# The second block's up stage with stationary weights, and matmuls of one size in a row

## The reference, cut to what matters

```python
# first block
h = rms_norm(x, ffn_norm_g)
a, g = jnp.split(h @ w_up, 2, axis=-1)           # 2048 x 11264
a = causal_dwconv(a, conv_w, conv_b)             # three taps along the rows
x = x + (gelu(a) * g) @ w_down
...
# second block
gu = rms_norm_2(x, norm_ffn) @ w_gate_up         # 2048 x 11264
gate, up = gu[..., :5632], gu[..., 5632:]
x = x + (silu(gate) * up) @ w_down_2
```

## Time and profile before

| | |
|---|---|
| median of 3 runs | 2599.71 us (2599.69 to 2600.31) |
| profiled execution | 2599.74 us, of it the span of the trace 2598.1 us |
| TensorE busy | 2586.1 us, 100% of the span |
| VectorE, ScalarE busy | 1474.3 us (57%), 1221.4 us (47%) |
| granted TensorE clock, mean | 0.999 |

### The profile page before, as it was taken

The page is one execution under the profiler, slowest core; times in us unless marked ns, Lnnn a source line. Parts: engine busy times, 40 slices in busy tenths (PEclk is TensorE's granted clock), DMA queues, the critical chain, the costliest instruction groups (busy, mean ns, idle before and its releaser), DMA issues.

```text
span 2598.1 us, 36344 instructions
## 1 busy us (share of the span) xinstructions
PE 2586.1 (100%) x12578; PEld 2182.8 (84%) x12578; DVE 1474.3 (57%) x1905; ACT 1221.4 (47%) x1568; POOL 74.4 (3%) x123
## 2 busy tenths in 40 slices
PE   9999999999999999999999999999999999999998
PEld 7889998888888888888887788888888888888887
DVE  5555665676666764445666655555545454454454
ACT  5544545555455544444554444444544444444433
POOL 2000000000000000001001100000000000000000
PEclk9999999999999999999999999999999999999999
DMA  7666666666666665566656556665666666665664
GB/s 214 188 170 166 163 177 197 189 185 184 185 190 186 184 192 190 192 190 203 187 167 194 156 184 193 189 192 186 186 189 187 191 185 193 189 190 191 207 194 154
DMA packets 359368, 483.79 MB, mean 186 GB/s; under 512 B 22984, under 2 KB 170640, under 8 KB 359024
## 3 DMA queue, kind: packets, MB, share of 16 engines
q1 hardware_dynamic: 352768, 476.13, 61.4%
q0 software_dynamic: 2112, 5.31, 0.8%
q10 hardware_dynamic: 4400, 1.19, 0.2%
HBM read 480.41 MB, written 2.14 MB: 186 GB/s over the span
## 4 chain that ended last, share of the span: by engine, by line
PE 99%; DMA 0%; DVE 0%; ACT 0%; issue 0%; SPq 0%; POOLq 0%; DVEq 0%; POOL 0%
PE acc L1491 25%; PE acc L1493 25%; PE acc L1492 25%; PE acc L1742 6%; PE acc L1743 3%; PE X L1742 3%; PE T L1742 3%; PE T L1743 2%; PE X L1743 2%; PE acc L1794 1%; PE acc L1792 1%; PE acc L1793 1%; PE T L1509 1%; PE acc L1745 0%; PE T L1726 0%; PE X L1887 0%
## 5 line engine op out<-in xcount | busy, mean ns | idle before, releaser
L881 DVE TENSOR_TENSOR wlo<-raw,whi 128x1024 fp32r<-128x1024 f32 (+1 forms) x916 | 1101.2, 1205 | 958.4 <-ACT whi L505 957.7
L505 ACT ACTIVATE whi<-raw 128x1024 fp32r<-128x1024 f32 (+1 forms) x916 | 949.8, 1044 | 1073.2 <-PE acc L1493 811.7
L1491 PE MATMUL acc<-whi,xt 128*128 128x512 f32 (+1 forms) x1472 | 565.2, 384 | 2.0 <-DVE wlo L881 2.0
L1493 PE MATMUL acc<-whi,xt 128*128 128x512 f32 (+1 forms) x1472 | 559.5, 380 | 0.0
L1492 PE MATMUL acc<-wlo,xt 128*128 128x512 f32 (+1 forms) x1472 | 558.9, 380 | 0.0
L1491 PEld LDWEIGHTS acc<-whi,xt 128*128 128x128 f32 x1472 | 276.4, 188 | 48.6 <-issue 2.1
L1493 PEld LDWEIGHTS acc<-whi,xt 128*128 128x128 f32 x1472 | 276.3, 188 | 47.9
L1492 PEld LDWEIGHTS acc<-wlo,xt 128*128 128x128 f32 x1472 | 276.5, 188 | 46.7
L1742 PE MATMUL acc<-xt,whi 128*128 128x512 f32 x660 | 247.7, 398 | 0.0
L1491 PE MATMUL acc<-whi,ht_hi 128*128 128x512 f32 x616 | 240.1, 390 | 0.0
L1493 PE MATMUL acc<-whi,ht_lo 128*128 128x512 f32 x616 | 239.7, 389 | 0.0
(11 more groups left out here) (324 smaller groups left out, 2605.9 us busy)
## 6 DMA issues: line engine op xcount, KB each, us to landing
raw<-in_w_up_dram SPq DMA_DIRECT2D x176, 512.0 KB, 3.7
raw<-in_w_down_dram SPq DMA_DIRECT2D x176, 512.0 KB, 4.6
raw<-in_w_gate_up_dram SPq DMA_DIRECT2D x176, 512.0 KB, 4.3
raw<-in_w_in_dram SPq DMA_DIRECT2D x256, 256.0 KB, 3.3
raw<-in_w_out_dram SPq DMA_DIRECT2D x64, 512.0 KB, 4.2
raw<-in_w_in_dram SPq DMA_DIRECT2D x64, 512.0 KB, 3.7
raw<-in_w_in_dram SPq DMA_DIRECT2D x128, 192.0 KB, 3.0
raw<-in_w_ple_gate_dram SPq DMA_DIRECT2D x32, 512.0 KB, 4.5
```

The lines of the kernel that those rows point to most:

```text
L505: act.activation(whi[:, s, :, 0:w.width], raw[:, s, :, 0:w.width], ACT.Copy).then_inc(hi_made, 1)
L881: dve.tensor_tensor(wlo[:, s, :, 0:w.width], raw[:, s, :, 0:w.width], whi[:, s, :, 0:w.width].bitcast(F32), ALU.subtract).then_inc(lo_made, 1)
L1491: pe.matmul(out_, h_, wh_, start=(j == 0 and kk == 0), stop=False)
L1493: done = pe.matmul(out_, l_, wh_, start=False, stop=(j == w.n - 1 and kk == KS - 1))
```

## The change

1. up2 goes over to `multiply_turned`, with the banks, evacuation, row factor, product and split of up. `glu_evac`, `glu_product`, `g_turn` and `glu_split` are gone. Silu is one ScalarE activation of 128x1024 from `a_part` into `hid` (`up2_silu`), behind stage 6 of window g. GpSimd sends the row factors of up2 through DRAM as well (`norm_row`, `row_back`).
2. In `multiply_turned` the 16 matmuls of a stage are grouped by size: an even stage runs eight of 512 columns and then eight of 256, an odd stage eight of 256 and then eight of 512. This holds for up and up2.

```diff
-        "up2": (FF // W, 16, 1, (FF // W, FF // W, 0, 0)),
+        "up2": (FF // W, 16, 1, (FF // W,) * 4),
...
+            def up2_silu(i):
+                act.wait_ge(a_scaled, i + (FFN0["up2"] + 1))
+                act.wait_ge(hid_lo, i + FFN0["up2"])
+                act.activation(hid[:], a_part, ACT.Silu).then_inc(hid_act, 1)
...
             def ffn_tail(phase, i):
-                return {6: [lambda: glu_split(i)]}
+                _, g = pair_windows(phase, i)
+                return {1: [lambda: up_gelu(i)] if phase == "up" else [],
+                        3: [lambda: up_low(phase, i, g, g_bank, g_part, g_low, hid_made)],
+                        6: [lambda: up_split(phase, i)]}
...
-                    hi(g, {3: [lambda: glu_evac(i, a)]})
+                    hi(g, {3: [lambda: up_low(phase, i, a, a_bank, a_part, a_low, hid_act)], 6: [lambda: up2_silu(i)]})
...
-                return {3: [lambda: glu_product(i, a, w)], 6: [lambda: glu_split(i)]}
+                return {4: [lambda: up_g(phase, i, w)], 5: [lambda: up_product(phase, i)], 6: [lambda: ffn_split(phase, i)]}
...
+                after = {4: [lambda: up_a(phase, i, a)]}
+                if phase == "up":
+                    after.update({5: [lambda: conv(i, 2)], 6: [lambda: conv(i, 1)], 7: [lambda: conv(i, 0)]})
...
-                    for kk in range(KS):
-                        k = KS * j + kk
-                        first, last = j == 0 and kk == 0, j == w.n - 1 and kk == KS - 1
-                        for c in range(4):
-                            cols_ = slice(c * P, (c + 1) * P)
-                            if not last:
-                                pe.matmul(blocks[c][:], whi[:, s, kk, cols_], xt[:, k].rearrange("p h c -> p (h c)"), start=first, stop=False)
-                            done = pe.matmul(blocks[c][:, 0:S], wlo[:, s, kk, cols_], xt_hi[:, k, :], start=False, stop=False)
-                            if last:
-                                done = pe.matmul(blocks[c][:], whi[:, s, kk, cols_], xt[:, k].rearrange("p h c -> p (h c)"), start=False, stop=True)
+                    def both_halves():
+                        for kk in range(KS):
+                            for c in range(4):
+                                done = pe.matmul(blocks[c][:], whi[:, s, kk, c * P:(c + 1) * P], xt[:, KS * j + kk].rearrange("p h c -> p (h c)"),
+                                                 start=(j == 0 and kk == 0), stop=(j == w.n - 1 and kk == KS - 1))
+                        return done
+
+                    def high_half():
+                        for kk in range(KS):
+                            for c in range(4):
+                                done = pe.matmul(blocks[c][:, 0:S], wlo[:, s, kk, c * P:(c + 1) * P], xt_hi[:, KS * j + kk, :],
+                                                 start=False, stop=False)
+                        return done
+
+                    if j % 2 == 0:
+                        both_halves()
+                        done = high_half()
+                    else:
+                        high_half()
+                        done = both_halves()
...
-            def ffn_tail(phase, i):
-                if phase == "up":
-                    return {}
-                return {3: [lambda: g_turn(i)]}
...
-            norm(NORM["out2"])
+            norm_row(NORM["out2"])
+            row_back(2)
```

More of the change, by code:

```diff
@@ L115, in sandwich_kernel @@
     T1, T2, X1, X2 = range(4)
+    FFN0 = {"up": 0, "up2": FF // W}
+    FFN_NORM = {"up": "out", "up2": "out2"}
     class Window:
@@ L333, in sandwich_kernel @@
         f_yhi = sem("f_yhi")
-        a_turned = sem("a_turned")
         rstd_stored = sem("rstd_stored")
@@ L347, in sandwich_kernel @@
         hid_lo = sem("hid_lo")
-        glu_hi = sem("glu_hi")
         p_landed = sem("p_landed")
@@ L682, in _, with up_low @@
             before = ws[-1]
-            def up_low(i, w, blocks, part, done, freed):
-                reached(act, freed, i)
+            def up_low(phase, i, w, blocks, part, done, freed):
+                reached(act, freed, i + FFN0[phase])
                 act.wait_ge(stage_used, w.end())
@@ L693, in up_gelu, with up_split @@
                 act.activation(hid[:], hid[:], ACT.Gelu).then_inc(hid_act, 1)
-            def up_split(i):
-                act.wait_ge(hid_made, i + 1)
-                act.activation(ht_hi[:, ds(4 * i, 4), :], hid[:], ACT.Copy).then_inc(hid_hi, 1)
[L699 to L711, removed]
-            def ffn_tail(phase, i):
-                if phase == "up":
-                    _, g = pair_windows(phase, i)
-                    return {1: [lambda: up_gelu(i)], 3: [lambda: up_low(i, g, g_bank, g_part, g_low, hid_made)],
-                            6: [lambda: up_split(i)]}
-                return {6: [lambda: glu_split(i)]}
+            def up2_silu(i):
+                act.wait_ge(a_scaled, i + (FFN0["up2"] + 1))
+                act.wait_ge(hid_lo, i + FFN0["up2"])
+                act.activation(hid[:], a_part, ACT.Silu).then_inc(hid_act, 1)
+            def up_split(phase, i):
+                act.wait_ge(hid_made, i + (FFN0[phase] + 1))
+                act.activation(ht_hi[:, ds(4 * i, 4), :], hid[:], ACT.Copy).then_inc(hid_hi, 1)
+            def ffn_tail(phase, i):
+                _, g = pair_windows(phase, i)
+                return {1: [lambda: up_gelu(i)] if phase == "up" else [],
+                        3: [lambda: up_low(phase, i, g, g_bank, g_part, g_low, hid_made)],
+                        6: [lambda: up_split(phase, i)]}
             def ffn(phase, i, pieces):
@@ L723, in ffn @@
                 if phase == "up":
-                    hi(g, {3: [lambda: up_low(i, a, a_bank, a_part, a_low, conv_done)]})
+                    hi(g, {3: [lambda: up_low(phase, i, a, a_bank, a_part, a_low, conv_done)]})
                 else:
-                    hi(g, {3: [lambda: glu_evac(i, a)]})
+                    hi(g, {3: [lambda: up_low(phase, i, a, a_bank, a_part, a_low, hid_act)], 6: [lambda: up2_silu(i)]})
             ffn("up", 0, residual("out", NB - 1, before, xt_hi, g_ffn))
@@ L1178, in _, with up_sum, up_a, up_g @@
             g_freed = [acc_read[1], acc_read[1], bank_read[T1], bank_read[T2]]
-            def up_sum(i, blocks, part, low, freed):
+            def up_sum(phase, i, blocks, part, low, freed):
                 for c in range(4):
-                    dve.wait_ge(low, 4 * i + c + 1)
+                    dve.wait_ge(low, 4 * i + (4 * FFN0[phase] + c + 1))
                     dve.tensor_tensor(part[:, c, :], blocks[c][:, 0:S], part[:, c, :], ALU.add).then_inc(freed[c], 1)
-            def up_a(i, a):
-                up_sum(i, a_bank, a_part, a_low, a_freed)
+            def up_a(phase, i, a):
+                up_sum(phase, i, a_bank, a_part, a_low, a_freed)
                 dve.wait_ge(acc_read[0], 2 * a.block + 2)
-                dve.wait_ge(bank_read[X2], USE0[X2]["up"] + i + 1)
-                dve.wait_ge(rstd_row_landed, 16)
+                dve.wait_ge(bank_read[X2], i + (USE0[X2][phase] + 1))
+                dve.wait_ge(rstd_row_landed, 16 if phase == "up" else 32)
                 dve.tensor_tensor(a_part, a_part, rstd_row[:].to_broadcast([P, 4, S]), ALU.mult).then_inc(a_scaled, 1)
-            def up_g(i, g):
-                up_sum(i, g_bank, g_part, g_low, g_freed)
+            def up_g(phase, i, g):
+                up_sum(phase, i, g_bank, g_part, g_low, g_freed)
                 dve.wait_ge(acc_read[1], 2 * g.block + 2)
-                dve.wait_ge(bank_read[T2], USE0[T2]["up"] + i + 1)
+                dve.wait_ge(bank_read[T2], i + (USE0[T2][phase] + 1))
                 dve.tensor_tensor(g_part, g_part, rstd_row[:].to_broadcast([P, 4, S]), ALU.mult).then_inc(g_scaled, 1)
@@ L1214, in conv, with up_product, ffn_split @@
                 done.then_inc(conv_done if tap == 0 else conv_step, 1)
-            def up_product(i):
-                dve.wait_ge(hid_act, i + 1)
-                dve.wait_ge(g_scaled, i + 1)
+            def up_product(phase, i):
+                dve.wait_ge(hid_act, i + (FFN0[phase] + 1))
+                dve.wait_ge(g_scaled, i + (FFN0[phase] + 1))
                 dve.tensor_tensor(hid[:], g_part, hid[:], ALU.mult).then_inc(hid_made, 1)
[L1221 to L1237, removed]
+            def ffn_split(phase, i):
+                dve.wait_ge(hid_hi, i + (FFN0[phase] + 1))
                 dve.tensor_tensor(ht_lo[:, ds(4 * i, 4), :], hid[:], ht_hi[:, ds(4 * i, 4), :].bitcast(F32), ALU.subtract)\
@@ L1242, in ffn_tail @@
                 a, w = pair_windows(phase, i)
-                if phase == "up":
-                    return {4: [lambda: up_g(i, w)], 5: [lambda: up_product(i)], 6: [lambda: ffn_split(i)]}
-                return {3: [lambda: glu_product(i, a, w)], 6: [lambda: glu_split(i)]}
+                return {4: [lambda: up_g(phase, i, w)], 5: [lambda: up_product(phase, i)], 6: [lambda: ffn_split(phase, i)]}
             def ffn(phase, i, pieces):
```

(33 more changed lines are left out.)

## The result

| | before | after |
|---|---|---|
| median | 2599.92 us (14 runs) | 2594.51 us (14 runs, 2594.36 to 2596.38) |
| ratio | | 0.9979, 95% interval 0.9972 to 0.9986 |
| span of the profiled execution | 2598.1 us | 2592.8 us |
| VectorE, ScalarE busy | 1474.3, 1221.4 us | 1524.6, 1243.9 us |

The kernel is 5.4 us faster, 0.21%. 8.0 had been forecast, 2591.7 us; the measured time lies in the range of 2582.5 to 2600, and 0.1 us outside the likeliest case's own 2589 to 2594.4. The gain is small, just over the 5.2 us (0.2%) that the forecast took as what a measurement can tell from no change, but the interval of the ratio stays under 1.

What follows compares the result with a forecast made beforehand. TensorE was taken as the bound, its start-to-start distances summed: up saves 7.5 to 8.1 us, up2 -0.1 to 0.5, together 7.4 to 8.6, middle 8.0. From 2599.71 that gives 2591.7 us, range 2582.5 to 2600.

Steps and rivals of the forecast that it cites:

- likeliest case: Whole kernel: a 256 follows a 256 after 119 to 121 ns, giving 2589 to 2594.4 us; chance 0.58.
- TensorE's pitches are the time: Whole kernel: time is the sum over TensorE's matmuls of the distance from one start to the next.
- 256 after 256 at 120 ns: Grouped runs in up and up2: each 256-column matmul starts 120 ns after the last; 2640 such steps.
- rival 2: Runs of 256s in both up stages: weight loads give way, each ns over 120 costs 2.6 us; chance 0.11.
- 13 ns to spare: Runs of 256s: a 128-column weight load was estimated at 106.7 ns, leaving 13 ns of each 120 spare.
- Rival 1: Both up stages: a 512 and a 256 cost 352.5 ns in any order, 7.6 us lost, 2607.3 us; chance 0.10.
- The two crossings of a round at 346.7 to 353.3 ns: Every two stages of up and up2: one size change each way, together 346.7 to 353.3 ns.
- 512 after 512 at 226.7 in both stages: Sign in the profile after: 512s follow each other at 226.7 ns in up and up2, else the forecast is wrong.
- a turn's 0.91 us: Up2 before the change: its transposes cost TensorE 0.91 us a pair, beside 43.52 us of matmuls.
- Up2: -0.1 to 0.5 us saved: Up2: 488.2 to 488.8 us after against 488.7 before, so -0.1 to 0.5 us saved.
- Four more fixed parts a stage: Up2: 16 matmuls a stage replace 12, adding 64 x 13.4 ns = 0.86 us, which pays back the turns' saving.
- The other engines at nothing: VectorE, ScalarE and GpSimd in up2: their changed work costs nothing, covered by TensorE.

Runs made afterwards that it cites:

- narrow_low: The full change with weights of 64 columns in place of 128 in the matmuls of 256, writing 64 result partitions in place of 128: 2577.99 us (one run).
- swap_only: Against the kernel before: up2 in its new form without turns, but 512 and 256 still in turn in both up stages: 2607.29 us, ratio 1.0030.

## Why the prediction was right, and what it missed

- *TensorE's pitches are the time.* Right: both up stages, to 0.1 us, make up the difference of the spans, and no wait came in.
- *256 after 256 at 120 ns.* Right, and rows 8 had carried it; this term decided the sum. What sets the 120 was not settled. It was read as 106.7 and a fixed 13.3 per matmul, with the load as a limit just below. The 13.3 isn't fixed: on weights 64 wide `narrow_low` shows 113, so 6.7 of it go with the width. That fits rival 2's mechanism, the load as the bound of a run, with its price already in the 120, but the runs don't show it. The 13 ns to spare that were worked out for the load are not shown either.
- *Rival 1, order makes no difference.* Fallen: the same matmuls in runs of 1 to 32 took 2592.5 to 2607.3 us. Its time for a swap without the gain, 2607.3, is what `swap_only` took, since there order was left as it was. The Trainium skill, TensorE: Matmul & The Clock Gate, section Back-to-back issue gap, gives a matmul's columns over 2.4 and 2.5 ns for a matmul by itself, and says that in a stream of loads and matmuls both set the spacing. The trace has 13.3 ns over the columns where that formula has 2.5 (226.7 ns at 512).
- *The two crossings of a round at 346.7 to 353.3 ns.* This is the term that was mis-sized. A crossing was priced as one couple. In fact a return to 512 makes five or so matmuls late, not one. A round came to (490.78 - 0.88) / 88 = 5.567 us, 16 ns above the middle of the forecast; over 176 rounds that is 2.8 us, and 2.6 are missing. By the forecast's own sign, 512 after 512 at 226.7 in both stages, this part was wrong: it holds for the later 512s of a run, not for the first five. Late 512s could have been read in the trace of before, behind up2's turns, where the shorter matmuls are transposes. Its timeline there:

```profile
1916.78 0.39 PE L1492 MATMUL acc<-wlo,xt 128*128 128x512 f32 x1
...
1917.94 0.39 PE L1491 MATMUL acc<-whi,xt 128*128 128x512 f32 x1
```

  Five steps in 1.16 us, 232 ns each, where 226.7 is steady. The forecast booked this as part of a turn's 0.91 us and didn't ask whether a return from 256 to 512 has it too.
- *Up2: -0.1 to 0.5 us saved.* Missed: 1.2 lost where the middle was 0.2 saved; 88 rounds at 16 ns are 1.4 us. "Four more fixed parts a stage" (0.86 us a pair) was the right sum for full weights, where 512, 384 and 256 all show some 13.3 ns over their columns; what the part consists of is open, as above.
- *The other engines at nothing.* Right: busy times within 0.5 us a pair, the late `whi` of 1.0 us in up2's pair 0 covered.
- *The gain, 8.0 us.* 5.4, two thirds of it. Right in sign, and nearly in place: 7.8 of the 8.0 were forecast in up, which gave 6.4, and up2 took 1.2 back. That the time fell inside the range owes something to its width: the range reached to the kernel before.

## What to carry to other kernels

When TensorE is the bound, cost a reordering by the distance from start to start, by which size follows which, and count several matmuls behind a return to the longer size. Splitting a change into its parts pays even where it won: here the small reordering carried the gain, and the large rewrite behind it cost 1.2 us. A run that changes two things at once, such as the width of the weights and of the result, shows that one of them matters and not which.

## What the runs showed of the hardware

- 256 moving columns on fp32r weights at the 2.4 GHz level: 120 ns from start to start with weights of 128 columns, 113 with 64. 512 columns: 226.7.
- Behind some changes of moving size, matmuls are late without any wait that the profile shows: 512s behind 256s 232 ns over the first six, 512s behind 384s 231 over the first eight, 384s behind 512s 178 over the first six. On full weights a 256 behind a 512 isn't late. With 256s it costs some 20 ns a round, whatever the run from 8 to 32, and the 512s are late also when the weights of the 256s are half as wide. Its cause the traces don't name.
- Runs of 2 (2595.6 us) beat runs of 4 (2602.6) and 8 (2597.7). The cause stays open.
